# Raw expert weights in a ring of ten, routing over half lists, readout spread over earlier stages, final norm joined to the next norm

## The reference, cut to what matters

```python
# first block: recurrent readout, merge, top-k experts, final norm
hn = h * rsqrt(mean(h*h, per head of 256) + EPS) * ml_norm
y_ml = sigmoid(z) * (hn + ml_skip * x_c)
out = (sigmoid(g_mla) * y_mla + sigmoid(g_ml) * y_ml) @ w_out
aff = softmax(x @ w_router)            # 1024 tokens x 16 experts
g, idx = top_k(aff.T, 128)             # per expert
y = (silu(xs @ w_gate) * (xs @ w_up)) @ w_down * g   # 16 experts, scatter-add
x = rmsnorm(x + g2 * y, final_norm)
# second block, layer 0 begins with
h = rmsnorm(x, norm_g) * (1 + scale) + shift ; h @ w_in
```

## Time and profile before

| | us |
|---|---|
| three runs | 3945.55, 3949.24, 4599.13 |
| median | 3949.24 |
| profiled execution | 3946.07 |
| its span, first to last instruction | 3944.3 |
| PE / DVE / ACT / POOL busy | 3344.9 / 1847.6 / 1476.2 / 642.9 |
| mean granted TensorE clock | 0.925 |

### The profile page before, as it was taken

How to read it: one execution, slowest core, us unless ns; L and a number is a source line. 1 busy time by engine, 2 the same in 40 slices (tenths; PEclk the granted TensorE clock), 3 DMA queues, 4 the chain that set the end, 5 groups by cost and what they waited for, 6 DMA issues and landing times. The chain is left out here.

```text
span 3944.3 us, 42824 instructions
## 1 busy us (share of the span) xinstructions
PE 3344.9 (85%) x17001; PEld 2701.3 (68%) x17001; DVE 1847.6 (47%) x2350; ACT 1476.2 (37%) x2225; POOL 642.9 (16%) x434
## 2 busy tenths in 40 slices
PE   6999998999996797674998988289988895998889
PEld 3777776777775586563777777168877774887767
DVE  3366783333334344647666667424323343152323
ACT  4223223343333344333666666331125314213531
POOL 2100000000000343212454544110000002000000
PEclk8999999999998899786999999589999997999999
DMA  5335652000000222335999999511130023113002
GB/s 193 95 118 179 198 179 71 13 20 18 13 13 3 105 105 82 116 120 196 341 337 341 331 344 325 208 43 52 35 102 15 1 86 117 52 48 100 15 5 92
DMA packets 235320, 475.87 MB, mean 121 GB/s; under 512 B 25475, under 2 KB 120580, under 8 KB 235124
## 3 DMA queue, kind: packets, MB, share of 16 engines
q1 hardware_dynamic: 219536, 415.26, 30.8%
q0 software_dynamic: 15264, 57.70, 4.4%
q10 hardware_dynamic: 324, 0.15, 0.0%
HBM read 410.50 MB, written 55.22 MB: 118 GB/s over the span
## 5 line engine op out<-in xcount | busy, mean ns | idle before, releaser
L2288 ACT ACTIVATE exp_wh<-wts_raw 128x2048 fp32r<-128x2048 f32 x192 | 367.7, 1917 | 289.1 <-DMA wts_raw<-in_w_e_down 99.1
L2328 DVE TENSOR_TENSOR exp_wl<-wts_raw,exp_wh 128x2048 fp32r<-128x2048 f32 x144 | 365.6, 2554 | 200.0 <-ACT exp_wh L2288 199.8
L2539 PE MATMUL pr_ps<-l_h_high,pr_wh 128*128 128x512 f32 (+1 forms) x896 | 335.8, 375 | 23.6 <-DVE pr_wl L2678 23.6
L2540 PE MATMUL pr_ps<-l_h_low,pr_wh 128*128 128x512 f32 (+1 forms) x896 | 330.7, 369 | 0.0
L2541 PE MATMUL pr_ps<-l_h_high,pr_wl 128*128 128x512 f32 (+1 forms) x896 | 329.9, 368 | 0.0
L729 PE MATMUL in_ps<-iw_h_high,in_wh 128*128 128x512 f32 (+1 forms) x696 | 274.1, 394 | 13.9 <-DVE in_wl L907 13.9
L2186 POOL TENSOR_TENSOR exp_wl<-wts_raw,exp_wh 128x2048 fp32r<-128x2048 f32 x48 | 230.5, 4803 | 330.6 <-ACT exp_wh L2288 330.6
L730 PE MATMUL in_ps<-iw_h_low,in_wh 128*128 128x512 f32 (+1 forms) x696 | 263.9, 379 | 0.0
L731 PE MATMUL in_ps<-iw_h_high,in_wl 128*128 128x512 f32 (+1 forms) x696 | 263.5, 379 | 0.0
L2678 DVE TENSOR_TENSOR pr_wl<-pw_raw,pr_wh 128x512 fp32r<-128x512 f32 x88 | 60.1, 692 | 358.2 <-ACT pr_wh L2600 356.8
L2539 PEld LDWEIGHTS pr_ps<-l_h_high,pr_wh 128*128 128x128 f32 x896 | 170.3, 190 | 54.9 <-DVE pr_wl L2678 24.1
(11 more groups left out here) (478 smaller groups left out, 7549.4 us busy)
## 6 DMA issues: line engine op xcount, KB each, us to landing
wts_raw<-in_w_e_gate SPq DMA_DIRECT2D x64, 1024.0 KB, 5.0
wts_raw<-in_w_e_up SPq DMA_DIRECT2D x64, 1024.0 KB, 4.9
wts_raw<-in_w_e_down SPq DMA_DIRECT2D x64, 1024.0 KB, 7.9
in_mw<-in_w_mod SPq DMA_DIRECT2D x80, 512.0 KB, 4.6
pw_raw<-in_w_in SPq DMA_DIRECT2D x88, 256.0 KB, 2.9
iw_raw<-in_w_in SPq DMA_DIRECT2D x74, 256.0 KB, 4.6
mod_w<-in_w_mod SPq DMA_DIRECT2D x4, 2048.0 KB, 11.7
wo_w<-in_w_out SPq DMA_DIRECT2D x2, 4096.0 KB
```

Source lines behind the costliest of these rows:

```text
L2288: act.activation(wh[:, m % RING], raw[:, m % RING], ACT.Copy).then_inc(high, 1)
L2328: dve.tensor_tensor(wl[:, m % RING], raw[:, m % RING], wh[:, m % RING].bitcast(F32), ALU.subtract).then_inc(low, 1)
L2539: nc.tensor.matmul(out, wh[:, slot, k, :], hi, start=h == 0 and k == 0, stop=False)
L2540: nc.tensor.matmul(out, wh[:, slot, k, :], lw, start=False, stop=False)
```

## The change

1. `attention`: SP and GpSimd no longer loop in hardware but have all eight heads written out. SP loads two more rows of 0.5 MB per head (`xc`, `s1`), and GpSimd does four instructions per head instead of one: xc times skip, times s1, y times sm, sum.
2. `mlstm`: ScalarE squares the finished tiles with running sums (32 instructions): the first four of each head's eight in the last four steps, each four steps late (`LATE`), the other four behind the first value eviction of the next head, and for the last head at the end.
3. `readout`: no squares and no skip term. VectorE scales the even tiles, ScalarE the odd ones. VectorE evicts the transposes straight with gain and gate in one instruction; the sum with the attention's part is GpSimd's for even tiles, VectorE's for odd ones. `s1` has eight buffers, the transposes four.
4. `route`: the affinities lie as two halves of 512, in rows 0 to 15 and 32 to 47 of one tile; 16 rounds run over both at once. The two sorted lists of 128 are merged by a comparison of the first with the second reversed (seven small VectorE instructions and four small matmuls instead of two copies and two transposes).
5. `experts`: `raw` has ten slots (`RAW_RING`); `wh` and `wl` keep four. Ten units are issued in `route`.
6. `moe_out` and the norm of layer 0 become one phase, `moe_out_normed`. GpSimd multiplies by `g2` and also makes the low part. The normed tile stays in SBUF and is stored to `g.xa` as well.

```diff
 # attention, GpSimd, per head
-                    pool.wait_ge(sm_in[j], (head - j) * 8 + 16)
+                    pool.wait_ge(sm_in[j], (head - j) * 24 + 48)
+                    x = xc[:, j:j + 1, :]
+                    pool.tensor_tensor(x, x, g.pa[...].to_broadcast([P, 1, N_LAT]), ALU.mult).then_inc(x_skip, 1)
+                    pool.wait_ge(x_skip, head + 1)
+                    pool.tensor_tensor(x, x, s1[:, j:j + 1, :], ALU.mult).then_inc(x_gated, 1)
                     pool.wait_ge(y_out, LT * (head + 1))
-                    pool.tensor_tensor(y, y, sm[:, j:j + 1, :], ALU.mult).then_inc(y_gated, 1)
+                    pool.tensor_tensor(y, y, sm[:, j:j + 1, :], ALU.mult).then_inc(y_mul, 1)
+                    ...
+                    pool.tensor_tensor(y, y, x, ALU.add).then_inc(y_gated, 1)
 # mlstm, ScalarE
+                def squares(head, m):
+                    act.wait_ge(added, head * (NO // 2) + m - NO // 2 + 1)
+                    ...
+                    act.activation(junk[:, sq_n[0] % 2], g.hs[...], ACT.Square, accum_out=g.ss[:, c, head:head + 1])
                     evict(head, V_USE)
+                    if head:
+                        for m in range(NO - LATE, NO):
+                            squares(head - 1, m)
                     ...
                         leave(head, m)
+                        if m - LATE >= NO // 2:
+                            squares(head, m - LATE)
+                for m in range(NO - LATE, NO):
+                    squares(ML_HEADS - 1, m)
 # readout, VectorE, per transposed tile
-                    dve.scalar_tensor_tensor(hn[:, t, :], xc[:, t % 2, :], skip, hn[:, t, :], ALU.mult, ALU.add)
-                    dve.tensor_tensor(hn[:, t, :], hn[:, t, :], s1[:, t % 2, :], ALU.mult).then_inc(gated, 1)
+                    dve.scalar_tensor_tensor(hn[:, t, :], tp[:, t % 4], gain, s1[:, t, :], ALU.mult, ALU.mult).then_inc(gated, 1)
+                    if t not in by_pool:
+                        dve.tensor_tensor(hn[:, t, :], hn[:, t, :], g.yT[:, t, :], ALU.add)
 # route
-        work = ph.sb("work", [N_EXP, 2, N_LAT])
+        work = ph.sb("work", [HALF_ROWS, 2, N_LAT // 2])
 # experts
-RING = 4
+RING, RAW_RING = 4, 10
-    sp.dma_start(g.raw[:, m % RING], src[u]).then_inc(g.raw_in[m % RING], 16)
+    sp.dma_start(g.raw[:, m % RAW_RING], src[u]).then_inc(g.raw_in[m % RAW_RING], 16)
-                        sp.wait_ge(*low_of(m - RING))
+                    sp.wait_ge(*low_of(m - RAW_RING))
```

More of the change, by code:

```diff
@@ L1808, in readout @@
 def readout(nc, g):
-    io = g.io
     with Phase(nc, "rdo") as ph:
[L1812 to L1819, removed]
+        ss, hn = g.ss, g.hn
+        s1 = ph.sb("s1", [P, KD, N_LAT])
+        tp = ph.ps("tp", [P, 4, 2, BANK])
+        names = ("var_done", "root_done", "inv_done", "even", "odd", "turned", "gated", "pooled")
+        var_done, root_done, inv_done, even, odd, turned, gated, pooled = (ph.sem(n) for n in names)
+        s1_in = [ph.sem(f"s1_in{t}") for t in range(KD)]
+        by_pool = [t for t in range(KD) if t % 2 == 0]
         with nc.Block() as block:
@@ new lines, in _ @@
+                for i in range(FIRST_LAT, FIRST_LAT + LOADS):
+                    load(i)
+                sp.dma_start(fn, spread(io["final_norm"])).then_inc(fn_in, 16)
+                prefetch(sp)
+                for n in range(LT):
+                    sp.wait_ge(xa_done, n + 1)
+                    sp.dma_start(g.xa[n * P:(n + 1) * P, :], xa[n % 2]).then_inc(stored[n % 2], 16)
+                    if n + LOADS < LT:
+                        load(FIRST_LAT + n + LOADS)
+                for j in range(2):
+                    sp.wait_ge(stored[j], 8 * LT)
@@ new lines, in modulated @@
+                def modulated(m):
+                    s = stream(m)
+                    dve.wait_ge(turned, m + 1)
+                    if m >= 2:
+                        dve.wait_ge(low_done, m - 1)
+                    for k in range(ACT_K, KD):
+                        ins = dve.tensor_scalar(y[:, m % 2, k, :], tp[:, m % SLOTS, 1, (k - 4) * P:(k - 3) * P],
+                                                gain[:, s, k:k + 1], mod[:, s, at_shift + k:at_shift + k + 1], ALU.mult, ALU.add)
+                    ins.then_inc(out_b, 1)
@@ new lines, in final @@
+                def final(i):
+                    n = i - FIRST_LAT
+                    if n == 0:
+                        dve.wait_ge(fn_in, 16)
+                    if n >= 2:
+                        dve.wait_ge(stored[n % 2], 16 * (n // 2))
+                    dve.scalar_tensor_tensor(xa[n % 2], x1[:, n % LOADS, :], inv[:, (i - 1) % 2, 0:1], fn, ALU.mult,
+                                             ALU.mult).then_inc(xa_done, 1)
+                for s in range(2):
+                    dve.scalar_tensor_tensor(gain[:, s, :], mod[:, s, at_scale:at_scale + KD], 1.0, norm,
+                                             ALU.add, ALU.mult).then_inc(gain_done, 1)
@@ new lines, in _ @@
+            @block.tensor
+            def _(pe):
+                for n in range(NT):
+                    pe.wait_ge(xn_done, n + 1)
+                    if n >= SLOTS:
+                        pe.wait_ge(out_a, n - SLOTS + 1)
+                        pe.wait_ge(out_b, n - SLOTS + 1)
+                    for k in range(KD):
+                        mm = pe.transpose(tp[:, n % SLOTS, k // 4, (k % 4) * P:(k % 4 + 1) * P],
+                                          x[:, n, k * P:(k + 1) * P], g.ident[:])
+                    mm.then_inc(turned, 1)
```

321 lines of the change are left out of this document (207 added, 114 removed).

## The result

The changed kernel takes 3839.24 us (median of 4 runs, 3835.86 to 3839.61), the kernel before 3949.9 us beside it: ratio 0.972, 95% interval 0.9705 to 0.9733, 110.7 us less. (One of the four runs of the kernel before fell in a slower state, with 4599.13 us, and the ratio is that of the others.) The forecast was 3859 in a range of 3808 to 3898, so the time lies in the range and on the faster side. The terms did not all come out as put, and one part of the likely explanation was incomplete.

What follows compares the result with a forecast made beforehand. It took PE and DMA as near their limits in the experts, late down weights causing waits, and VectorE as holding routing. Terms -48 - 24 - 34 + 6 + 4 + 8 = -88 against 3946.07 gave 3858, 3859 with offset; range 3808 to 3898.

Steps and rivals of the forecast that it cites:

- Experts: Expert stage: longer load ring removes PE's hidden-tile wait, 40.2 to 37.2 us per expert, minus 48 us (bounds 25 to 60).
- DMA floor: Expert stage: at 2.81 us per unit an expert needs 37.8 us of DMA, 36.7 with the units in store.
- Six more units in store, 1.1 per expert: Expert stage: six more units loaded at the start save 16.9 us of DMA, 1.1 per expert.
- Rival (b): Expert stage: VectorE and GpSimd together hold it, up to 39.3 us per expert; gain 15 instead of 48, 3892 us; chance 0.17.
- Rival (d): Expert stage: scatters land behind ten queued units, 47 us per expert, plus 109, 4015 us in all; chance 0.02.
- Routing: Routing: rounds over half the columns save 25.4 us, merging the lists costs 1.6; minus 24 us (bounds 22 and 25).
- readout: Readout: squares go, scaling is shared, tile pairs take 4.84 us; 30.3 against 64.7 us, minus 34 (bounds 28 and 40).
- Recurrent stage: Recurrent stage: four squares at each of three head borders delay PE's next eviction; plus 6 us (bounds 1 and 9).
- Attention: Attention: last head ends with two GpSimd instructions instead of one, 2.34 us, other bursts mostly covered; plus 4 us.
- Rival (c): Attention: GpSimd's bursts at head borders hold up VectorE, costing 37 us instead of 4, 3892 us in all; chance 0.10.
- Joined phase: Final norm with next norm: VectorE and GpSimd exclude each other, 9.9 us per tile, 105 against 96.7 us; plus 8.
- Rival (a): Joined phase: GpSimd and VectorE run side by side, minus 29 in place of plus 8, 3822 us; chance 0.12.

Runs made afterwards that it cites:

- e1: The changed kernel with the raw weight ring at four slots (RAW_RING = 4) in place of ten; 3911.12 us, ratio 0.9881.
- e5: The changed kernel without the product with the weights' low part, and VectorE's and GpSimd's low parts made over half of each unit; 3791.88 us, ratio 0.9598.
- e2: The changed kernel with the raw weight ring at six slots (RAW_RING = 6) in place of ten; 3839.85 us, ratio 0.9691.
- e3: The changed kernel with one of PE's three expert products left out, the one with the tokens' (or hidden tile's) low part; 3846.28 us, ratio 0.9706.
- e8: The changed kernel with each head's four late squares placed ahead of ScalarE's first eviction of values in the recurrent stage; 3836.47 us, ratio 0.9715.
- e9: The changed kernel without attention's skip path (both products, the sum and two loads per head left out); 3849.42 us, ratio 0.9721.
- e7: The changed kernel with GpSimd's product by g2 and low part of the joined phase both moved to VectorE; 3822.22 us, ratio 0.9675.

## Why the prediction was right, and where it wasn't

**Experts: the wait was the right one, a term was mis-sized.** The forecast said that late down weights hold up ScalarE, that ScalarE's hidden tile stands behind them, and that a longer ring removes 48 us. The idle time of PE fell by 48.4 us, and e1 brings it back. What failed is the step "PE needs 580.7 / 16 = 36.3 us, part of it at the lower clock level (mean 0.96)": I saw the lower clock and took it as fixed. It goes with the waits. With them gone PE needs 563.1 / 16 = 35.2 us, and e1 returns both together. Gate to last down product came to 577.2 us, not 595. That the idle time came out at 48.4 against 48 is partly luck: the 37.2 us per expert were PE's 37.0 and something for late DMA or VectorE, and the DMA floor beside it was wrong.

**Experts: the DMA floor was wrong.** "DMA allows 36.7 us" would have held the stage at 587 us; it is 577.2, and e5 shows 33.3. The 2.81 us per unit were busy share times time, taken from a queue that ran short at times; the same working gives 2.62 in e5, so the share isn't pure work. What else it counts, no run shows. "Six more units in store, 1.1 per expert" was wrong too: e2 has two more and is as fast. What counts seems to be the bridge over a wait of at most 5.2 us, two units of 2.7; a ring of five was not tried.

**Rival (b), VectorE and GpSimd together,** got its place right and its price wrong. They are the next bound, but at 36.4 us per expert (e3), not 39.3: VectorE's four other instructions per expert read an operand from PSUM and lie beside GpSimd's low parts unhindered. In e3 the weighting of the down product overlaps a low part of GpSimd's in 15 of 16 experts and takes at most 1.285 us; in the kernel before it does so in 14 of 16 and takes at most 1.283, so the trace of before could have priced this rival. The 36.4 are no fixed limit either, since the changed kernel with more work for PE takes 36.1. So its stage lies within some 3% of two limits at once, PE with 563 of 577.6 us busy and the pair VectorE and GpSimd, with DMA behind them, at 533 us if e5 is a guide.

**Rival (d), scatters behind ten units,** fell at its root. A scatter lands in 12.3 us with ten slots, as in the 12.5 of the earlier trace rows with four.

**Routing, readout.** Both as put. MAX8 takes 0.69 us, as the elementwise instruction of 512 columns in the earlier trace rows said; the merge of the lists ends 4.2 us after the last round (1776.2 to 1780.4) against an allowance of 1.6 on top of the old end, so 22.7 came in place of 24. The readout came to 28.9, forecast 30.3: a pair takes 4.7 us, the 4.84 of the working less what the second scaling does beside GpSimd.

**Recurrent stage.** Forecast 6, measured 6.2, by the mechanism named: PE's wait at the border of heads grew from 0.27 to 1.71 us, where 1.5 more was forecast, and e8 takes 5.1 away with one line moved.

**Attention.** Forecast 4. Of the 6.7 us in the table 2.0 lie ahead of head 0's gating, a point that moves between 738.4 and 741.7 in the eleven runs (739.0 in the kernel before); 2.1 are the step to the sixth head, which only some of the executions show; 2.6 are left for the skip path, and e9 gives 2.7 to 3.3. That is the last head's sum of 2.34, as put, and little besides. Rival (c) fell.

**Joined phase.** Forecast +8, measured +1.0. The step that failed is the tile of 9.9 us: it is 9.02. I added all parts in full, one behind the other. In the trace they overlap a little at every joint: the low part starts before VectorE's final product ends (2411.54 against 2411.71), and of GpSimd's product, 2.80 us long, VectorE waits 2.24. Over the six steady tiles that is 5.3 us less than put. The rest of the 105 didn't come out either, and cancels in part. From the phase's first instruction to the third sum, where the steady tiles begin, 24.8 us pass in place of 8 + 12. Behind them 18.3 us are left in place of 22 + 4; 2.6 of these are a slip in the sum, since 9.9 less GpSimd's 2.34 and the sum's 1.22 is 6.3 per tile and not 7.2. So 97.2 us in place of 105 is the net of -5.3, +4.8 and -7.7, and that it lies so near is in part luck. The lock itself is as the forecast had it. The scaling stands at 2.85 us beside GpSimd and 0.75 without it, and e7 shows what it was worth: 20 us for moving GpSimd's work to the engine that was already the busier one. Rival (a), that the two run side by side, is false for instructions with two SBUF inputs and for the plain scaling; it is true for an instruction with one operand in PSUM, as the readout's second scaling shows. The rule of the Trainium skill that the forecast weighed (page "SBUF — State Buffer", section "Who interferes with whom") says all three of these (of the scaling, that it can enter a two-port mode), and each is borne out here.

The sum of the forecast's terms was -88 against -106.6 in the spans. The 18.6 between them are the experts' 17.9 and a remainder in which the other rows nearly cancel.

## What to carry to other kernels

When a wait of PE goes away, price its busy time at the clock it will have without the wait, not at the clock of the old trace: read the granted clock of the stage beside a stretch in which PE never waits. A DMA share near 1 (1.02, 1.01 and 1.03 in three kernels here) doesn't say that DMA is the limit, and a consumer that waits for a landing doesn't either: ScalarE did so in the kernel before, where the ring was short and SP waited 354.7 of 400 us for slots. Both together say it, late landings and an issuer that seldom waits for a slot (107.1 us in e5). A ring doesn't have to be long: two more slots did here what six did. Where VectorE is the bound beside GpSimd, moving GpSimd's elementwise work to VectorE can shorten the phase, since each of these GpSimd instructions cost VectorE 2.1 to 2.2 us (2.85 in place of 0.75, and a wait of 2.24) where doing the work itself costs 1.22. Before calling two engines exclusive, look for the instructions that keep their duration beside the other engine: those are free.

## What the hardware showed that I had not expected

- The same 2546 matmul records took 580.7 us with 62.9 us of waits between them (clock 0.96), 563.1 us with 14.5 us of waits (0.99), and 583.0 again when the waits were put back in e1.
- The time of all DMA engines per unit of 1.049 MB isn't a constant: 2.81 us before, 2.70 in the changed kernel, 2.62 in e5, where the rate over 400 us is 397 GB/s, with slices of up to 416.
- One step in attention takes 78.6 to 79.1 us in some executions and 80.6 to 80.8 in others of the same code, at a granted clock of 0.98 in place of 1.00. The merge does the same: 143.7 and 144.0 us at 0.88 in the two profiles of the changed kernel, 145.6 to 146.0 at 0.86 in the ten edited ones, whose code is the same there; what decides it, no run shows. A difference of 2 us between two profiles of this kernel needs a third profile.
- In e3 PE has a third less to do and a mean clock of 0.91. It is busy 448 us, not the 380 that two thirds of 563 would give.
